# Key stages with both halves of the input side by side, and the bank's halves added on VectorE

## The chip, the cores and the metric

The kernel runs on one core of a Trainium2 chip. The metric is the device time of one execution in microseconds (us), as the median of several runs. A tile is 128 partitions high throughout; 512 f32 columns of the accumulation memory are one bank.

## The reference

Two transformer-like blocks are applied one after the other to 256 tokens of width 1024, in f32. The change is in the PEER layers of the first block, of which there are two (layer 0 and layer 1):

```python
def peer(h, w_q, sub_keys, u_emb, v_emb):
    # per block of 128 tokens x_t
    q = einsum('td,dhk->thk', x_t, w_q).reshape(T, 8, 2, 128)
    s = einsum('thpk,hpnk->thpn', q, sub_keys)
    sv, si = top_k(s, 16)                       # 16 best of 128 keys, for both halves
    cand = sv[:, :, 0, :, None] + sv[:, :, 1, None, :]
    fv, fpos = top_k(cand, 16)                  # 16 best of 256 sums
    gate = softmax(fv)
    act = gelu(einsum('thkd,td->thk', u_emb[eidx], x_t), approximate=False)
    return einsum('thk,thkd->td', gate * act, v_emb[eidx])
```

There are 16384 experts of width 1024 in each layer. The kernel does not gather the chosen rows: it computes the activation of every expert for every token, multiplies by a table of gates that is zero for experts not chosen, and multiplies the result with the whole of `v_emb`.

## The kernel before

f32 products are made of reduced-precision parts. A 128 x 1024 weight tile that arrives in `weight_raw` is rounded by ScalarE into `weight_high` (`make_high`, L272), and VectorE writes raw minus high over the raw tile as `weight_low` (`make_low`, L278). The input `h` is kept as `h_high` and `h_low` in the same way. A product (`product`, L382) is three matmuls: high weight with high input, high weight with low input, low weight with high input. There are four weight slots and four banks in use (`RING` = 4). SyncE loads tile n as soon as TensorE has finished tile n - 4 (`tiles_used`).

The stage that is changed is `peer_scores` (called the key stage here). It runs once in each layer, over 128 tiles of 128 experts. For every tile TensorE makes 8 blocks of three matmuls of 256 columns into one half of a bank, waiting for the weight's low part and for the bank (`bank_free`). What the others do in one step of the order written out by hand:

- ScalarE, step n: wait until tile n is multiplied (`tiles_used`); Gelu of bank n into `acts` (L1227), which also frees the bank; `make_high` of tile n + 3. After nine of the steps in a layer the Exp of a head's gates follows (L1236). In layer 0, after every fourth step from 15 on, it issues the DMA of a modulation block of 512 KB (`load_later_modulation`, L683), i.e. the one that VectorE uses in the next step of its own that has one. The first two blocks are loaded by SyncE at the start.
- VectorE, step n (from 3 on): `make_low` of tile n, which waits for `make_high` of tile n. In layer 0, where n >= 10 and n % 4 == 2, then one block of modulation work (L654, 128 x 1024), which waits for that block's DMA; 28 of them in the stage. In nine steps the sum, reciprocal and product for a head's gates (L1261 to L1263). Then as many of the 256 picking steps (`pick_experts`: 16 steps for each of 8 heads and two token groups) as are due: `done * PICKED_BY < n * 256`.
- GpSimd scatters the gates of seven heads to the table in HBM, one indirect DMA for each of 16 picks and head.

Each of these queues is executed strictly in this order. Behind the key stage lies `peer_weigh`, which builds what multiplies the second token group's activations, and `peer_output`, which multiplies with `v_emb` by matmuls of 512 columns (L1442).

The lines used below: L272 high part, L278 low part, L382 the matmuls of `product`, L592 `add_to_x` (VectorE adds a bank to an SBUF tile), L321 Square of such a tile on ScalarE, L654 and L683 modulation work and its DMA, L1087 to L1145 the picking, L1227 Gelu, L1236 Exp, L1442 the 512-column matmuls of the output stage.

Of the kernel before, what the change touches and what calls it, by code (L numbers as in the profile page):

```python
# [8 lines left out]
F32R = mybir.dt.float32r  # L9
I32 = mybir.dt.int32  # L10
U32 = mybir.dt.uint32
ALU = mybir.AluOpType
# [3 lines left out]
P = 128  # L16
D = 1024
KB = D // P
T = 256
# [142 lines left out]
class Core:  # L162


    def __init__(self, nc, dram):
        self.nc, self.dram = nc, dram
        sb = lambda name, shape, dt=F32: nc.alloc_sbuf_tensor(name, shape, dt)
        aligned = lambda: (nc.sbuf_base + 31) // 32 * 32

        def over(name, shape, dt, start):  # L170

            return nc.alloc_sbuf_tensor_at(name, shape, dt, offset=start)

        arena_at = aligned()
        self.arena = sb("arena", [P, P * T])
        self.x = sb("x_T", [P, KB, T])


        h_at = aligned()
        self.h_high = sb("h_high", [P, KB, T], F32R)  # L180
        self.h_low = sb("h_low", [P, KB, T], F32R)

        self.scratch = over("scratch", [P, 2 * KB * T], F32, h_at)
        self.act_high = over("act_high", [P, RING, T], F32R, h_at)
        self.act_low = over("act_low", [P, RING, T], F32R, h_at + RING * T * 4)

        self.mem_high = over("mem_high", [P, KB, T], F32R, arena_at + 4 * MEM_AT)
        self.mem_low = over("mem_low", [P, KB, T], F32R, arena_at + 4 * (MEM_AT + KB * T))

        self.hidden_high = over("hidden_high", [P, 32, T], F32R, arena_at + 4 * 10240)  # L190
        self.hidden_low = over("hidden_low", [P, 32, T], F32R, arena_at + 4 * 18432)

        raw_at = aligned()
        self.raw = sb("weight_raw", [P, RING, KB * P])
        self.low = over("weight_low", [P, RING, KB * P], F32R, raw_at)
        high_at = aligned()
        self.high = sb("weight_high", [P, RING, KB * P], F32R)

        self.spare = over("spare", [P, RING, KB * P], F32, high_at)
        self.work = sb("work", [P, 512])  # L200
        self.squares = sb("squares", [P, 2, T])
        self.kept = sb("kept", [P, 16 * T])
        self.kv = view(self.kept, 0, 16, T)
        self.later = view(self.kept, 0, 2, D)
        self.mem = view(self.kept, 0, KB, T)
        self.silu = self.kept[:, 2 * D:3 * D]
        self.gates = view(self.kept, 3 * D, RING, P)
        self.table = [nc.dram_tensor(f"gate_table{layer}", (P * P * P, 1), F32, kind="Internal").ap() for layer in range(2)]
        self.const = sb("const", [P, dram["resident"].shape[1]])
        self.cols = sb("cols", [P, dram["cols"].shape[1]])  # L210
        self.mod = sb("mod", [P, 2, 48])
        self.gain = sb("gain", [P, 4, KB])
        self.trig = sb("trig", [P, 4, T])
        self.pick = Picks(sb, self.kept[:, 3 * D + RING * P:4 * D].rearrange("p (t a b) -> p t a b", t=TT, a=TOPK))
        self.banks = nc.alloc_psum_tensor("bank", [P, 8 * BANK], F32)
        self.bank = [self.banks[:, i * BANK:(i + 1) * BANK] for i in range(8)]
        self.flags = {}
        self.segments = []
        self.next_segment = 0

    def sig(self, name):
        if name not in self.flags:
            self.flags[name] = Signal(self.nc, name)
        return self.flags[name]
# [151 lines left out]
    def product(self, out, slot, rhs, k, start, stop):  # L376
# [5 lines left out]
            mm = self.nc.tensor.matmul(out, w, x, start=(start and i == 0), stop=(stop and i == 2), skip_group_check=skip)  # L382
        return mm


    def linear(self, engine, take, groups=1, rhs=None, loads=(), aside=None, per_tile=1, norm=None, squares=None, root=None, aside_act=None, halves=None, first=None):

# [675 lines left out]


PICK_STEPS = 16
PICKED_BY = 104
GATED_BY = 112


def picked_at(h):  # L1070
# [112 lines left out]
def peer_scores(core, layer):  # L1183
# [2 lines left out]

    nc, sig = core.nc, core.sig
    used, free, step, picked = sig("tiles_used"), sig("bank_free"), sig("dve_step"), sig("experts_picked")
    exped, gated, turned, cleared = sig("gates_exped"), sig("gates_ready"), sig("turned"), sig("table_cleared")
    seg, k = core.take_segment()  # L1190
    following = core.segments[k + 1]
# [6 lines left out]
    with nc.Block() as block:  # L1198
        @block.sync
        def _(sp):  # L1200
            if layer == 0:
                sp.wait_ge(cleared.sem, 16 * CLEARINGS)
                for n in range(EARLY_MODS, EARLY_MODS + 2):
                    load_later_modulation(core, sp, n)
            core.stream(sp, seg, k)

        @block.tensor
        def _(pe):
            with pe.Fori(0, P // RING) as turn:
                for slot in range(RING):  # L1210

                    pe.wait_ge(free.sem, turn * RING + free.at(slot + 1 - RING))
                    core.wait_turn(pe, seg, turn, slot)
                    for c in range(KB):
                        mm = core.product(core.bank[slot][:, 0:T], slot, (core.h_high[:, c, :], core.h_low[:, c, :]), c,
                                          c == 0, c == KB - 1)
                    mm.then_inc(used.sem, 1)

            pe.wait_ge(gated.sem, gated.at(HEADS + 1))
            transposes(core, pe, [b.chosen[:, 1, 1, :]], [core.bank[4]], turned)  # L1220
            transposes(core, pe, [b.expo[:, 1].rearrange("p h k -> p (h k)")], [core.bank[5]], turned)

        @block.scalar
        def _(act):
            for n in range(P):
                act.wait_ge(used.sem, seg.first + RING + n + 1)
                nc.scalar.activation(acts[:, n, :], core.bank[n % RING][:, 0:T], ACT.Gelu).then_inc(free.sem, 1)  # L1227
                ahead = n + RING - 1
                if ahead < P:
                    core.make_high(act, seg, ahead - ahead % RING, ahead % RING)  # L1230
                else:
                    core.make_high(act, following, 0, ahead - P)
                if ahead in exp_at:
                    h = exp_at[ahead]
                    act.wait_ge(picked.sem, picked.at(h + 1))
                    nc.scalar.activation(gates(h), gates(h), ACT.Exp).then_inc(exped.sem, 1)  # L1236
                if layer == 0 and n % RING == RING - 1 and 3 <= n // RING < LATER // 2 + 3:
                    load_later_modulation(core, act, EARLY_MODS + n // RING - 1)

        @block.gpsimd  # L1240
        def _(pool):
            pool.wait_ge(cleared.sem, 16 * CLEARINGS * (layer + 1))
            scatter_gates(core, pool, layer, range(SCATTERED_EARLY))

        @block.vector
        def _(dve):

            link = Chain(step, dve)
            picking = (i for t in range(TT) for h in range(HEADS) for i in pick_experts(core, link, scores, t, h))
            steps = modulations(core, dve, range(EARLY_MODS, EARLY_MODS + LATER // 2))  # L1250
            done, all_steps = 0, TT * HEADS * PICK_STEPS
            for n in range(RING - 1, P):
                core.make_low(dve, seg, n - n % RING, n % RING)
                if layer == 0 and n >= 10 and n % RING == 2:
                    next(steps, None)
                if n in gate_at:
                    h = gate_at[n]
                    total = b.total[:, 0:1] if h < HEADS else b.total[:, HEADS:2 * HEADS]
                    of = gates(h)
                    dve.wait_ge(exped.sem, exped.at(h + 1))  # L1260
                    link(nc.vector.tensor_reduce(total, of, AX_X, ALU.add))  # L1261
                    link(nc.vector.reciprocal(total, total))
                    nc.vector.tensor_tensor(of, of, total.unsqueeze(2).to_broadcast(list(of.shape)), ALU.mult) \  # L1263
                        .then_inc(gated.sem, 1)
                while done < all_steps and done * PICKED_BY < n * all_steps:
                    next(picking)
                    done += 1
            step.used = link.n
            for n in range(RING - 1):
                core.make_low(dve, following, 0, n)  # L1270
            for n in range(2):
                dve.wait_ge(turned.sem, turned.at(n + 1))
                nc.vector.tensor_copy(b.by_pick[:, n, :], core.bank[4 + n][:, 0:P])
# [2 lines left out]
    picked.close(HEADS + 1)  # L1276
    exped.close(HEADS + 1)
    free.close(P)


WEIGHED_EARLY = 2
# [1426 lines left out]
```

## Time and profile before

| | value |
|---|---|
| median of 3 runs | 2740.25 us (2738.56 to 2741.69) |
| the profiled execution | 2738.82 us, of which the traced span is 2736.7 us |
| key stage of layer 0, from the low part of tile 3 to the last low part | 380.4 us |
| key stage of layer 1, the same | 366.1 us |
| mean granted TensorE clock | 0.965 of 2.4 GHz |

Of the page, part 1 is the busy time of each engine, part 2 the same in 40 slices of 68.4 us, and part 5 the groups of instructions. The two key stages lie in slices 4 to 9 and 19 to 24 (counted from 1): there TensorE (PE) is the busiest and VectorE (DVE) second. The busy time of PE counts overlapping matmuls once.

### The profile page before, as it was taken

The page shows a single profiled execution, that of the slowest core. Times are in us where ns is not written, and L with a number is a line of the kernel's source. Part 1 is how long each engine was busy: PE and PEld are TensorE (multiplying, and loading weights), DVE is VectorE, ACT ScalarE, POOL GpSimd, SP SyncE. Part 2 cuts the span into 40 slices and gives each one's busy share as a digit, 9 for nine tenths or more (in the row PEclk, how much of TensorE's full clock was granted, in tenths as well). Part 3 has the DMA queues.
Part 4 walks back from the last instruction along what each step waited for, and adds up shares of the span by engine and source line. Part 5 has one row for each costly group of instructions (what it writes and reads, how often), then busy time and mean ns, then how long its engine had stood idle before and what let it go on. Part 6 is the DMA issues. An engine that isn't in the chain of part 4 may idle for free. (4 is left out here: it accounts for less than half of the span.)

```text
span 2736.7 us, 45422 instructions
## 1 busy us (share of the span) xinstructions
PE 2511.7 (92%) x17052; PEld 2287.0 (84%) x17052; DVE 1858.1 (68%) x3789; ACT 1308.0 (48%) x1979; POOL 508.6 (19%) x320
## 2 busy tenths in 40 slices
PE   5698999999999999778999998999999988888998
PEld 4588999997888889468999997788888867777998
DVE  5676998858777774654888848666665566554754
ACT  3345554556444454344665456455545441044443
POOL 0001666623000000100576743000000010000000
PEclk8899999999999999789999999999999989999999
DMA  8755777762787765334777762677774530033554
GB/s 347 266 174 153 220 210 220 218 215 39 255 265 268 262 215 166 147 97 135 184 182 180 184 184 43 209 217 217 218 216 132 161 109 24 1 118 95 163 163 154
DMA packets 200510, 480.75 MB, mean 176 GB/s; under 512 B 54448, under 2 KB 87728, under 8 KB 199760
## 3 DMA queue, kind: packets, MB, share of 16 engines
q1 hardware_dynamic: 150960, 432.01, 49.9%
q10 hardware_dynamic: 12576, 47.29, 4.4%
q0 software_dynamic: 36864, 0.15, 3.4%
q8 instruction: 48, 0.79, 0.1%
q14 instruction: 62, 0.51, 0.1%
HBM read 461.41 MB, written 17.96 MB: 175 GB/s over the span
## 5 line engine op out<-in xcount | busy, mean ns | idle before, releaser
L278 DVE TENSOR_TENSOR weight_low<-weight_raw,weight_high 128x1024 fp32r<-128x1024 f32 x732 | 892.3, 1221 | 405.2 <-ACT weight_high L272 397.1
L272 ACT ACTIVATE weight_high<-weight_raw 128x1024 fp32r<-128x1024 f32 x732 | 773.9, 1059 | 663.8 <-DMA weight_raw<-peer_v_dram 336.8
L382 PE MATMUL bank<-h_high,weight_high 128*128 128x256 f32 x3424 | 984.0, 287 | 81.1 <-DVE weight_low L278 24.2
L382 PE MATMUL bank<-h_low,weight_high 128*128 128x256 f32 x3424 | 979.3, 286 | 0.0
L382 PE MATMUL bank<-h_high,weight_low 128*128 128x256 f32 x3424 | 978.9, 286 | 0.0
L382 PEld LDWEIGHTS bank<-h_high,weight_high 128*128 128x128 f32 x3424 | 668.3, 195 | 95.1 <-issue 80.8
L382 PEld LDWEIGHTS bank<-h_low,weight_high 128*128 128x128 f32 x3424 | 668.2, 195 | 0.0
L382 PEld LDWEIGHTS bank<-h_high,weight_low 128*128 128x128 f32 x3424 | 667.9, 195 | 0.0
L1161 POOL DMA_INDIRECT gate_table<-pick_expo,pick_spot x256 | 468.6, 1831 | 752.1 <-DVE pick_expo L1263 461.1
L1442 PE MATMUL bank<-weight_high,act_high 128*128 128x512 f32 x1024 | 316.6, 390 | 6.1 <-DVE act_low L1509 6.1
L1442 PE MATMUL bank<-weight_low,act_high 128*128 128x512 f32 x1024 | 316.8, 391 | 0.0
L1442 PE MATMUL bank<-weight_high,act_low 128*128 128x512 f32 x1024 | 316.2, 390 | 0.0
L1509 DVE TENSOR_TENSOR act_low<-arena,act_high 128x256 fp32r<-128x256 f32 x256 | 108.7, 424 | 213.5 <-ACT act_high L1476 212.8
L1442 PEld LDWEIGHTS bank<-weight_high,act_high 128*128 128x128 f32 x1024 | 192.6, 188 | 46.4 <-issue 6.4
L1442 PEld LDWEIGHTS bank<-weight_high,act_low 128*128 128x128 f32 x1024 | 193.1, 189 | 40.3
L1442 PEld LDWEIGHTS bank<-weight_low,act_high 128*128 128x128 f32 x1024 | 193.1, 189 | 40.1
L1227 ACT ACTIVATE arena<-bank 128x256 f32<-128x256 f32 x256 | 97.9, 383 | 224.0 <-PE bank L382 222.2
L1598 POOL TENSOR_TENSOR arena<-arena,trig 128x512 f32<-128x512 f32 x12 | 17.9, 1524 | 487.8 <-POOLq L398 487.8
L1476 ACT ACTIVATE act_high<-arena 128x256 fp32r<-128x256 f32 x256 | 102.3, 400 | 12.3 <-PEq L1301 11.6
L585 ACT ACTIVATE arena<-bank 128x256 f32<-128x256 f32 x108 | 41.2, 381 | 130.9 <-PE bank L382 130.9
L654 DVE SCALAR_TENSOR_TENSOR kept<-kept 128x1024 f32<-128x1024 f32 x56 | 68.4, 1221 | 25.0 <-DMA kept<-ada_later_dram 24.9
L1596 POOL MEMSET kept<- 128x1024 f32 x1 | 1.0, 951 | 454.1 <-SPq L1565 454.1
(342 smaller groups left out, 2691.8 us busy)
## 6 DMA issues: line engine op xcount, KB each, us to landing
weight_raw<-peer_u_dram SPq DMA_DIRECT2D x256, 512.0 KB
weight_raw<-peer_v_dram SPq DMA_DIRECT2D x256, 512.0 KB
kept<-ada_later_dram ACTq DMA_DIRECT2D x54, 512.0 KB
gate_table<-kept ACTq DMA_DIRECT2D x8, 2048.0 KB, 16.7
weight_raw<-peer_w_q_dram SPq DMA_DIRECT2D x32, 512.0 KB
kept<-gate_table SPq DMA_DIRECT2D x256, 64.0 KB, 3.4
weight_raw<-w_in_dram SPq DMA_DIRECT2D x32, 512.0 KB
weight_raw<-mlp_w_up_dram SPq DMA_DIRECT2D x32, 512.0 KB
```

Source lines behind the costliest of these rows:

```text
L272: self.nc.scalar.activation(self.high[:, slot, :], self.raw[:, slot, :], ACT.Identity) \
L278: eng.tensor_tensor(self.low[:, slot, :], self.raw[:, slot, :], self.high[:, slot, :].bitcast(F32), ALU.subtract) \
L382: mm = self.nc.tensor.matmul(out, w, x, start=(start and i == 0), stop=(stop and i == 2), skip_group_check=skip)
L585: return lambda n, bank: self.nc.scalar.activation(dst[:, n + offset, :], bank, func)
L654: i = nc.vector.scalar_tensor_tensor(out=block, in0=block, scalar=1.0, in1=core.silu[:], op0=ALU.mult, op1=ALU.mult, accum_out=mod[:, n:n ...
L1161: pool.indirect_dma_start(core.table[layer], bass.IndirectOffsetOnAxis(ap=b.spot[:, h, i:i + 1], axis=0), b.expo[:, 0, h, i:i + 1], None, ...
L1227: nc.scalar.activation(acts[:, n, :], core.bank[n % RING][:, 0:T], ACT.Gelu).then_inc(free.sem, 1)
L1442: mm = nc.tensor.matmul(out[2 * t + h][:], x[:, slot, of], w[:, slot, halves[h]], start=(first and n == 0), stop=(last and n == 2), skip_g ...
L1476: nc.scalar.activation(core.act_high[:, n % RING, :], acts[:, n, :], ACT.Identity).then_inc(rounded.sem, 1)
L1509: nc.vector.tensor_tensor(core.act_low[:, slot, :], acts[:, n, :], core.act_high[:, slot, :].bitcast(F32), ALU.subtract).then_inc(split.se ...
L1596: nc.gpsimd.memset(core.later[:, 0, :], 0.0).then_inc(sig("zeros_made").sem, 1)
L1598: nc.gpsimd.tensor_tensor(dst[:, 2 * n:2 * n + 2, :], src[:, 2 * n:2 * n + 2, :], cosb, ALU.mult) \
```

## The change

`h_high` and `h_low` become two views of one tile `h_parts`, in which the high and the low half of each of the 8 blocks of the input lie side by side: 512 columns. In the key stages the two matmuls with the high weight become one of 512 columns over the whole bank; the matmul with the low weight has 256 columns and adds to the bank's first half. In the last block of a tile the narrow one comes first. The two halves of a bank then have to be added: ScalarE copies the second half to `acts` (a new semaphore `halves_copied`), VectorE adds the first half to it, which frees the bank, and ScalarE's Gelu now works on `acts` in SBUF, one step later. `PICKED_BY` goes from 104 to 116 and `GATED_BY` from 112 to 122.

```diff
-        self.h_high = sb("h_high", [P, KB, T], F32R)
-        self.h_low = sb("h_low", [P, KB, T], F32R)
+        self.h_parts = sb("h_parts", [P, KB, 2, T], F32R)
+        self.h_high, self.h_low = self.h_parts[:, :, 0, :], self.h_parts[:, :, 1, :]
...
+    def side_by_side(self, bank, slot, k):
+
+        high, low = self.high[:, slot, k * P:(k + 1) * P], self.low[:, slot, k * P:(k + 1) * P]
+        parts, last = self.h_parts[:, k], k == KB - 1
+        wide = lambda: self.nc.tensor.matmul(bank[:], high, parts.rearrange("p s t -> p (s t)"), start=(k == 0), stop=last,
+                                             skip_group_check=True)
+        narrow = lambda: self.nc.tensor.matmul(bank[:, 0:T], low, parts[:, 0, :], start=False, stop=False, skip_group_check=True)
+        if last:
+            narrow()
+            return wide()
+        wide()
+        return narrow()
...
-PICKED_BY = 104
-GATED_BY = 112
+PICKED_BY = 116
+GATED_BY = 122
...
                     for c in range(KB):
-                        mm = core.product(core.bank[slot][:, 0:T], slot, (core.h_high[:, c, :], core.h_low[:, c, :]), c,
-                                          c == 0, c == KB - 1)
+                        mm = core.side_by_side(core.bank[slot], slot, c)
...
         @block.scalar
         def _(act):
+            def activate(n):
+                act.wait_ge(free.sem, free.at(n + 1))
+                nc.scalar.activation(acts[:, n, :], acts[:, n, :], ACT.Gelu)
+
             for n in range(P):
                 act.wait_ge(used.sem, seg.first + RING + n + 1)
-                nc.scalar.activation(acts[:, n, :], core.bank[n % RING][:, 0:T], ACT.Gelu).then_inc(free.sem, 1)
+                nc.scalar.activation(acts[:, n, :], core.bank[n % RING][:, T:2 * T], ACT.Identity).then_inc(copied.sem, 1)
+                if n:
+                    activate(n - 1)
                 ahead = n + RING - 1
                 if ahead < P:
                     core.make_high(act, seg, ahead - ahead % RING, ahead % RING)
...
+            activate(P - 1)
...
+            def add(n):
+                dve.wait_ge(copied.sem, copied.at(n + 1))
+                nc.vector.tensor_tensor(acts[:, n, :], core.bank[n % RING][:, 0:T], acts[:, n, :], ALU.add).then_inc(free.sem, 1)
+
             for n in range(RING - 1, P):
                 core.make_low(dve, seg, n - n % RING, n % RING)
+                add(n - RING + 1)
...
             for n in range(RING - 1):
                 core.make_low(dve, following, 0, n)
+                add(P - RING + 1 + n)
```

## Rows read from the trace of the kernel before

**Rows 1.** Windows: both key stages, then 100 us of layer 1's key and output stages.

```profile
core 0: us, PE busy (x) PEld busy (x) DVE busy (x) ACT busy (x) POOL busy (x), PEclk, DMA share, GB/s
230.88:611.32 380.44, 369.40 (x3039) 365.44 (x3037) 319.66 (x828) 205.46 (x281) 209.41 (x112) 1.00 0.75 214
1288.58:1654.68 366.10, 364.59 (x3039) 364.35 (x3037) 286.72 (x772) 206.26 (x281) 209.41 (x112) 1.00 0.72 182
...
1400.00:1500.00 100.00, 100.00 (x835) 100.00 (x835) 85.60 (x249) 56.71 (x78) 68.06 (x37) 1.00 0.74 181
...
1800.00:1900.00 100.00, 100.00 (x443) 82.81 (x442) 65.44 (x114) 51.76 (x78) 0.00 (x0) 1.00 0.71 217
```

**Rows 2.** Waits in layer 0's key stage: who waited for whom, total us, times, longest.

```profile
DVE kept L654 <- DMA kept<-ada_later_dram: 24.9, 23, 2.2
```

**Rows 3.** Timeline of both engines in a later stage that adds banks to SBUF.

```profile
2438.84 1.06 ACT L272 ACTIVATE weight_high<-weight_raw 128x1024 fp32r<-128x1024 f32 x1 [1.23 <-DMA weight_raw<-xattn_w_q_dram]
...
2439.93 1.22 DVE L278 TENSOR_TENSOR weight_low<-weight_raw,weight_high 128x1024 fp32r<-128x1024 f32 x1 [0.70 <-ACT weight_high L272]
2441.08 0.41 DVE L330 TENSOR_TENSOR work<-work,squares 128x256 f32<-128x256 f32 x1
2441.41 0.42 DVE L592 TENSOR_TENSOR x_T<-bank,x_T 128x256 f32<-128x256 f32 x1
...
2441.86 0.42 ACT L321 ACTIVATE squares<-x_T 128x256 f32<-128x256 f32 x1 [1.65 <-DVE x_T L592]
```

**Rows 4.** Instructions by line: duration min/median/max in ns, of Square from SBUF.

```profile
L321 ACT ACTIVATE squares<-x_T x40: 397/401/418, 133.3 to 2728.4; 128x256 f32<-128x256 f32 x40
```

**Rows 5.** Timeline of VectorE in layer 1's key stage (start, duration, line, form).

```profile
1289.72 0.48 DVE L1087 MAX8 pick_top<-arena 128x8 f32<-128x128 f32 x2
...
1293.87 1.21 DVE L278 TENSOR_TENSOR weight_low<-weight_raw,weight_high 128x1024 fp32r<-128x1024 f32 x1
```

**Rows 6.** Timeline around an Exp, layer 1's key stage: ScalarE, and VectorE behind it.

```profile
1345.07 0.21 ACT L1236 ACTIVATE pick_expo<-pick_expo 128x16 f32<-128x16 f32 x1
1345.30 1.28 ACT L1227 ACT_TABLE_LOAD   x1
1346.59 0.38 ACT L1227 ACTIVATE arena<-bank 128x256 f32<-128x256 f32 x1
1346.87 1.05 ACT L272 ACTIVATE weight_high<-weight_raw 128x1024 fp32r<-128x1024 f32 x1
...
1348.03 1.23 DVE L278 TENSOR_TENSOR weight_low<-weight_raw,weight_high 128x1024 fp32r<-128x1024 f32 x1 [1.54 <-ACT weight_high L272]
```

**Rows 7.** Timeline, layer 0: three modulation blocks, the DMA's issue and VectorE's use.

```profile
419.74 0.34 ACTq L683 DMA_DIRECT2D kept<-ada_later_dram  x1
...
425.17 1.23 DVE L654 SCALAR_TENSOR_TENSOR kept<-kept 128x1024 f32<-128x1024 f32 x1 [1.92 <-DMA kept<-ada_later_dram]
...
493.18 0.33 ACTq L683 DMA_DIRECT2D kept<-ada_later_dram  x1
...
497.01 1.23 DVE L654 SCALAR_TENSOR_TENSOR kept<-kept 128x1024 f32<-128x1024 f32 x1 [0.51 <-DMA kept<-ada_later_dram]
...
575.84 1.06 ACT L272 ACTIVATE weight_high<-weight_raw 128x1024 fp32r<-128x1024 f32 x1 [0.34 <-DMA weight_raw<-peer_u_dram]
575.85 0.33 ACTq L683 DMA_DIRECT2D kept<-ada_later_dram  x1
...
580.13 1.22 DVE L654 SCALAR_TENSOR_TENSOR kept<-kept 128x1024 f32<-128x1024 f32 x1 [1.98 <-DMA kept<-ada_later_dram]
```

**Rows 8.** Windows with TensorE partly idle, and the clock granted in them.

```profile
2328.00:2340.00 12.00, 9.04 (x115) 8.58 (x112) 7.01 (x13) 0.00 (x0) 3.83 (x16) 1.00 0.01 2
...
609.00:621.00 12.00, 8.08 (x45) 6.95 (x44) 7.85 (x22) 7.95 (x15) 6.18 (x4) 0.86 0.28 64
```

**Rows 9.** Timeline of TensorE: the idle stretch behind layer 0's key stage.

```profile
613.79 0.48 PE L1322 MATMUL bank<-spread_by,pick_firsts 128*128 128x512 f32 x1 [3.92 <-ACT spread_by L1345]
```

More of the change, by code:

```diff
@@ L1188, in peer_scores @@
     used, free, step, picked = sig("tiles_used"), sig("bank_free"), sig("dve_step"), sig("experts_picked")
+    copied = sig("halves_copied")
     exped, gated, turned, cleared = sig("gates_exped"), sig("gates_ready"), sig("turned"), sig("table_cleared")
@@ L1278, in peer_scores @@
     free.close(P)
+    copied.close(P)
 WEIGHED_EARLY = 2
```

## The prediction

> **What bounds the kernel now.** I read the page's slices first: both key stages show TensorE full and VectorE at 60 to 90%. Then the windows [rows 1]. In layer 1's key stage TensorE is busy 364.6 of 366.1 us at the full clock of 2.4 GHz: it is the bound. 835 matmuls of 256 columns in 100 us are 119.8 ns each, so a tile of 24 takes 2.874 us, and 127 tiles 365 us. In layer 0 the stage is 380.4 us long with the same matmuls; VectorE is busy 319.7 us there, against 286.7, because of 28 modulation blocks, and it also waits 23 times, 24.9 us in all, for their DMA [rows 2]. VectorE is near its limit there, and the stage is bound by TensorE in some tiles and by VectorE in others. The GpSimd scatter is busy 209 us of either and ends before it.
>
> What matters most is not in any busy share: how the queues hang together. Before, ScalarE's step n needs only TensorE's tile n and a loaded weight; VectorE's step needs ScalarE's high part. Nothing on ScalarE waits for VectorE, but for an Exp that follows its picks by two tiles. So an engine that falls behind in one tile can catch up in the next.
>
> **TensorE's part of the change.** A matmul of 512 columns costs 100 us / 443 = 225.7 ns [rows 1] (in the output stage, same reduced-precision type, full clock). A block is then 225.7 + 119.8 = 345.5 ns instead of 359.3, a tile 2.764 us instead of 2.874: 0.110 us less, 14 us in each layer, if TensorE remained the bound. The Trainium skill ("TensorE: Matmul & The Clock Gate", section "Wait — 56ns, not 53.3ns?") gives a fixed cost of about 2.5 ns for each matmul at the full clock, by which the saving would be 2.5 ns x 8 x 128 x 2 = 5 us in all. The rows say otherwise: two narrow ones minus one wide are 13.9 ns, and I go by them.
>
> **The new loop.** ScalarE's step m is now: copy of bank m, Gelu of m - 1, high part of m + 3. That Gelu waits for VectorE's addition m - 1, which stands in VectorE's queue behind the low part of m + 2, which waits for the high part of m + 2, which stands behind ScalarE's Gelu of m - 2. So one turn of a ring through both engines is needed for each tile, and no buffer loosens it. Its terms, from a stage where the same forms follow each other [rows 3]: low part to the start of the next on VectorE 1.15 us (2439.93 to 2441.08, I take 1.14); addition from a bank 0.42; end of it to the start on ScalarE 0.03 to 0.05 (2441.83 to 2441.86); Gelu from SBUF as Square from SBUF, 0.40 [rows 4], of which 0.10 overlaps the next instruction: 0.30 (Gelu from a bank shows 0.28 to the next high part [rows 6]); high part 1.06; to VectorE 0.03 (2439.90 to 2439.93). I take 0.04 and 0.06 for the two crossings, as one in the key stage is 0.11 (1347.92 to 1348.03) [rows 6]. Sum 1.14 + 0.42 + 0.04 + 0.30 + 1.06 + 0.06 = **3.02 us**, over TensorE's 2.76. The loop takes the bound: 127 turns are 383.5 us. TensorE isn't in it: tile m is multiplied some 4.1 us after the start of its low part, and the copy of it has until 5.9 us (two turns less 0.1). The copy itself (0.28 to the next instruction) lies in ScalarE's gap of 1.66 us while VectorE makes low part and addition, and costs nothing; with that gap gone it would cost 0.28.
>
> **What hangs on VectorE.** After the addition has started, VectorE has 3.02 - 1.14 - 0.34 = 1.54 us for the rest before the next high part is there. Picking: the first 8 steps take 1289.72 to 1293.87 = 4.15 us [rows 5]. In all of layer 1's stage VectorE is busy 286.7 us [rows 1], 156 of it with 128 low parts of 1.22; with the 0.04 us that a step waits for its forerunner, some 250 times, the 256 steps are 141 us. The rule gives 7 steps in the first tile (3.7 us of work, +2.2 us over a turn), then two or three a tile, 1.21 us on average. They fit but where three long ones meet: +3.2 us by going through the schedule. PICKED_BY at 116 costs nothing by itself, as the gates for the last transposes are due at 122 of 128.
>
> **Exp.** Nine times in a layer ScalarE puts a table load of 1.28, the Exp of 0.21 and another table load of 1.28 into its queue (the Exp and the load behind it stand in [rows 6]). Before, that was covered by ScalarE's idle time. Now 1.28 + 0.24 + copy 0.28 + 1.28 = 3.08 must fit in the gap of 1.66: 1.42 over, x 9 = +12.8 us. The bounds are 0 (the loads elsewhere) and that.
>
> Layer 1: 383.5 + 2.2 + 3.2 + 12.8 = **401.7** against 366.1, +35.6 us.
>
> **Modulation blocks in layer 0.** Block i is asked for in ScalarE's step 4i + 7, behind the high part of tile 4i + 10, and used in VectorE's step 4i + 10. The last one: issue 575.85, use 580.13, 4.28 us later; two earlier ones, with the scatter beside them, took 5.43 (419.74 to 425.17) and 3.83 us (493.18 to 497.01), the longest and the shortest of the 23 that were waited for [rows 7]. VectorE waited 1.1 us on average before, since it was otherwise behind ScalarE and the block had had time. In the loop it is never behind: the issue comes with the Gelu's start, 1.40 us before the low part starts, and VectorE is ready for the block 1.48 after. With 4.5 us for the DMA it waits until 3.10, 1.62 us each. A tile with a block takes 3.10 + 1.15 + 1.21 = 5.46 instead of 3.02: +2.44, x 26 = 63.4 us; the two blocks loaded at the start cost 0.8 each, 1.6. Less what coincides (three of the Exp excesses 4.3, picks that are already counted 0.7, the last block without picks 1.3): 58.7. Layer 0: 401.7 + 58.7 = **460.4** against 380.4, +80.0 us.
>
> **Ends.** The next stage starts 0.3 us later than before in relation to the last low part (one addition), the first tile is 0.1 us shorter, in both layers: +0.4. The strided `h_high` and `h_low` elsewhere are rows of 256 as before: 0. Sum: 80.0 + 35.6 + 0.4 = **+116 us**, from the profiled 2738.8 to 2854.8; that execution lies 1.4 us under the median. I predict 2855.
>
> **Bounds.** Crossings at 0.03 both: -6 us, at 0.11 both: +20. DMA at 3.8: -18, at 5.4: +23. Exp hidden: -20. The forecast's own range is 2830 to 2890.
>
> **Rivals.**
> 1. The loop holds but the modulation DMA is hidden (it lands within 2.9 us, because less is moved in a us): tile with a block 1.48 + 1.15 + 1.21 = 3.84, layer 0 about 421, time 2738.8 + 40 + 36 = 2815 to 2818. Against it: no block of the trace was used under 3.8 us after its issue where VectorE waited. Chance 0.12.
> 2. Faster: TensorE stays the bound. It decides when a turn of the loop is under 2.76 us, that is if 0.26 us of its terms overlapped across engines; then 14 us go in each layer, 2711. For it speaks only that TensorE is the bound now and has less to do; against it, every term is a row, and semaphores put them in sequence. Also here lies the case that it is near zero because the loop costs what the matmuls save. Chance 0.04 faster, 0.02 even. In layer 0 the modulation would undo it in part.
> 3. The clock. TensorE would be busy 2.76 of 3.0 to 5.5 us, idle up to 2.7 at a time. The rows have 75% busy at full clock, and a fall after an idle stretch of 3.92 us [rows 8, 9]. If it fell in a third of layer 0's tiles, a tile there takes 8 x (225.7 + 119.8) x 2 = 5.5 us, about 1.9 over the mean 3.6: +80 us, 2935. The Trainium skill (the same page, "A second HAM failure mode: psum-queue depth-cycling") describes a clock that oscillates where TensorE idles briefly between groups; the rows here don't bear that out for gaps under 3 us. Chance 0.09.
> 4. The wide matmul isn't cheaper than two narrow ones: TensorE's tile stays 2.87, still under 3.02, and nothing changes in the time. It is inside the forecast.
>
> **Chances.** Forecast 0.70 (2830 to 2890), hidden DMA 0.12, clock 0.09, faster 0.04, even 0.02, slower otherwise 0.03. The range for 8 in 10 takes in the first two: 2812 to 2890. A difference under 0.2% (5.5 us) can't be told from none: faster 0.04, same 0.02, slower 0.94.
>
> **What would show it.** In the profile after: 512-column matmuls at 226 ns apart, gaps of TensorE before each tile that end with the low part; the low parts 3.0 us apart in layer 1 with VectorE waiting for the high part and ScalarE's Gelu waiting for the addition (about 1.2 us each time); 4.4 us where an Exp lies; in layer 0 every fourth interval over 5 us, with VectorE waiting about 40 us in all for `kept<-ada_later_dram`; stages of about 460 and 402 us. Wrong if the low parts follow each other by less than 2.9 us, if the modulation wait doesn't grow, or if the granted clock in the stages is under 1.00.

## The result and the profile after

The changed kernel takes 2863.48 us (median of 4, 2858.77 to 2864.55) against 2740.92; the ratio is 1.0445, 95% interval 1.0427 to 1.0463. The profiled execution took 2864.51 us, with a span of 2862.7 us, 126.0 more than before.

The first view is the windows of both key stages, from the low part of tile 3 to the last one, and of 100 us inside layer 1's, as in [rows 1]. Columns: us, then busy time (and instructions) of PE, PEld, DVE, ACT and POOL, the granted clock, DMA share and GB/s.

```profile
231.26:693.87 462.61, 391.67 (x2026) 321.09 (x2025) 363.46 (x954) 234.97 (x409) 198.49 (x112) 0.96 0.63 177
1376.85:1779.29 402.44, 382.13 (x2028) 308.40 (x2026) 329.24 (x898) 234.39 (x409) 195.68 (x112) 1.00 0.65 167
1450.00:1550.00 100.00, 92.39 (x489) 74.09 (x488) 84.67 (x244) 61.63 (x106) 68.36 (x41) 1.00 0.67 160
```

Layer 0's stage grew from 380.4 to 462.6 us (+82.2), layer 1's from 366.1 to 402.4 (+36.3). That is 118.5 of the 126.0. TensorE has gaps now, VectorE has more work but isn't full (329 of 402 us), and ScalarE is busy 58% of the time in layer 1. TensorE is still shown as busy 95% of layer 1's stage, but that alone doesn't make it the bound: e5 below lengthens its work on a tile, and the stage stays as it is. What binds, only the waits show. These are the largest of layer 1's stage between the engines of the chain, and then the ones of layer 0's; GpSimd's waits and those of the weight loads are left out (us in total, times, longest):

```profile
ACT arena L1240 <- DVE arena L1274: 164.4, 116, 1.9
DVE weight_low L278 <- ACT weight_high L272: 71.2, 81, 7.5
```

```profile
ACT arena L1240 <- DVE arena L1274: 227.2, 119, 4.5
PE bank L390 <- DVE weight_low L278: 65.4, 38, 3.1
DVE weight_low L278 <- ACT weight_high L272: 56.4, 66, 7.4
DVE kept L667 <- DMA kept<-ada_later_dram: 40.9, 26, 2.1
```

ScalarE's Gelu (now L1240) waits for VectorE's addition (L1274), and VectorE's low part for ScalarE's high part: two engines that wait for each other in turn. Before, the Gelu waited for TensorE (222.2 us in both layers). The wait for the modulation DMA grew from 24.9 us [rows 2] to 40.9. Some turns of the ring in layer 1, first VectorE's lines, then ScalarE's:

```profile
1502.21 1.23 DVE L278 TENSOR_TENSOR weight_low<-weight_raw,weight_high 128x1024 fp32r<-128x1024 f32 x1 [0.23 <-ACT weight_high L272]
1503.35 0.42 DVE L1274 TENSOR_TENSOR arena<-bank,arena 128x256 f32<-128x256 f32 x1
...
1505.28 1.23 DVE L278 TENSOR_TENSOR weight_low<-weight_raw,weight_high 128x1024 fp32r<-128x1024 f32 x1 [0.56 <-issue]
```

```profile
1503.81 0.42 ACT L1240 ACTIVATE arena<-arena 128x256 f32<-128x256 f32 x1 [1.43 <-DVE arena L1274]
1504.13 1.04 ACT L272 ACTIVATE weight_high<-weight_raw 128x1024 fp32r<-128x1024 f32 x1
1505.08 0.36 ACT L1244 ACTIVATE arena<-bank 128x256 f32<-128x256 f32 x1
1506.87 0.42 ACT L1240 ACTIVATE arena<-arena 128x256 f32<-128x256 f32 x1 [1.43 <-DVE arena L1274]
```

Low part 1502.21, addition 1503.35 to 1503.77, Gelu 1503.81, high part 1504.13 to 1505.17, next low part 1505.28: 3.07 us. The profile names no releaser for the wait before that last one (`issue`), but the high part had ended 0.11 us before it. These are the same terms as were taken from [rows 3], in a stage where they formed no ring.

### The profile page after: what moved, and what is told of

It is laid out like the page before. It is cut to its first block and busy times, and to the rows that moved or that the text cites. A ratio compares the mean times of both kernels' runs of the same rounds, so it can differ in the third digit from the quotient of the medians.

```text
span 2862.7 us, 41854 instructions
## 1 busy us (share of the span) xinstructions
PE 2556.2 (89%) x15004; PEld 2186.5 (76%) x15004; DVE 1945.4 (68%) x4045; ACT 1363.5 (48%) x2235; POOL 484.6 (17%) x320
## 5 line engine op out<-in xcount | busy, mean ns | idle before, releaser
L390 PE MATMUL bank<-h_parts,weight_high 128*128 128x512 f32 x2048 | 766.4, 412 | 94.8 <-DVE weight_low L278 79.1
L1174 POOL DMA_INDIRECT gate_table<-pick_expo,pick_spot x256 | 444.1, 1735 | 898.4 <-DVE pick_expo L1288 467.9
L382 PE MATMUL bank<-h_parts,weight_high 128*128 128x256 f32 x2752 | 516.6, 290 | 58.0 <-DVE h_parts L548 20.8
L390 PEld LDWEIGHTS bank<-h_parts,weight_high 128*128 128x128 f32 x2048 | 391.0, 192 | 226.9 <-issue 140.6
L392 PE MATMUL bank<-h_parts,weight_low 128*128 128x256 f32 x2048 | 540.6, 284 | 0.0
L382 PEld LDWEIGHTS bank<-h_parts,weight_high 128*128 128x128 f32 x2752 | 444.7, 199 | 68.7 <-issue 61.3
L392 PEld LDWEIGHTS bank<-h_parts,weight_low 128*128 128x128 f32 x2048 | 395.9, 193 | 13.7
L382 PE MATMUL bank<-h_parts,weight_low 128*128 128x256 f32 x1376 | 397.7, 289 | 0.0
L1240 ACT ACTIVATE arena<-arena 128x256 f32<-128x256 f32 x256 | 107.1, 418 | 394.9 <-DVE arena L1274 391.6
L382 PEld LDWEIGHTS bank<-h_parts,weight_low 128*128 128x128 f32 x1376 | 272.9, 198 | 0.0
L1469 PEld LDWEIGHTS bank<-weight_high,act_low 128*128 128x128 f32 x1024 | 193.4, 189 | 40.3
L1503 ACT ACTIVATE act_high<-arena 128x256 fp32r<-128x256 f32 x256 | 102.3, 400 | 12.3 <-PEq L1328 11.6
L1274 DVE TENSOR_TENSOR arena<-bank,arena 128x256 f32<-128x256 f32 x256 | 107.0, 418 | 0.0
L598 ACT ACTIVATE arena<-bank 128x256 f32<-128x256 f32 x108 | 41.3, 382 | 132.1 <-PE bank L382 132.1
```

Of the source, the lines that this page charges most:

```text
L390: wide = lambda: self.nc.tensor.matmul(bank[:], high, parts.rearrange("p s t -> p (s t)"), start=(k == 0), stop=last, skip_group_check=True)
L392: narrow = lambda: self.nc.tensor.matmul(bank[:, 0:T], low, parts[:, 0, :], start=False, stop=False, skip_group_check=True)
L598: return lambda n, bank: self.nc.scalar.activation(dst[:, n + offset, :], bank, func)
L1174: pool.indirect_dma_start(core.table[layer], bass.IndirectOffsetOnAxis(ap=b.spot[:, h, i:i + 1], axis=0), b.expo[:, 0, h, i:i + 1], None, ...
L1240: nc.scalar.activation(acts[:, n, :], acts[:, n, :], ACT.Gelu)
L1274: nc.vector.tensor_tensor(acts[:, n, :], core.bank[n % RING][:, 0:T], acts[:, n, :], ALU.add).then_inc(free.sem, 1)
```

## The experiments

Stage lengths are read as above in each kernel's own trace, from the low part of tile 3 to the last low part. All are variants of the changed kernel, but e6, which is one of the kernel before. Stages are of one profiled execution each.

| kernel | layer 0's stage | layer 1's stage | median us |
|---|---|---|---|
| before | 380.4 | 366.1 | 2740.9 |
| changed | 462.6 | 402.4 | 2863.5 |
| e1_high_first | 420.7 | 358.5 | 2774.4 |
| e2_mod_early | 422.3 | 402.4 | 2820.9 |
| e3_no_tables | 456.8 | 390.8 | 2845.0 |
| e5_narrow_halves | 464.9 | 402.4 | 2864.1 |
| e8_short_gelu | 458.9 | 391.8 | 2844.7 |
| e7_both | 379.5 | 358.6 | 2732.3 |
| e4_wide_alone | 372.7 | 358.5 | 2725.5 |
| e6_before_mod_early | 367.5 | 366.1 | 2727.9 |
| e9_layer1_only | 365.9 | 358.3 | 2718.8 |
| e10_wide_early | 360.2 | 358.4 | 2712.4 |

**Breaking the ring (e1_high_first).** Two instructions change places in ScalarE's order:

```diff
                 nc.scalar.activation(acts[:, n, :], core.bank[n % RING][:, T:2 * T], ACT.Identity).then_inc(copied.sem, 1)
-                if n:
-                    activate(n - 1)
                 ahead = n + RING - 1
                 if ahead < P:
                     core.make_high(act, seg, ahead - ahead % RING, ahead % RING)
                 else:
                     core.make_high(act, following, 0, ahead - P)
+                if n:
+                    activate(n - 1)
```

> The changed kernel, but in ScalarE's step n the high part of tile n + 3 is issued ahead of the Gelu of tile n - 1. Theory (a ring of Gelu, high part, low part, addition, one turn of 3.02 us for each tile): the ring then spans two tiles, some 1.6 us each, and no longer binds. TensorE's 2.76 us and VectorE's 2.69 us of own work do: layer 1's stage about 355 us instead of 402.4, layer 0's about 390 instead of 462.6 (modulation DMA still partly waited for), the whole about 2745 us. Rival (VectorE is simply full with the additions, or the wide matmuls are slow): the order on ScalarE changes little, over 2830 us.

2774.4 us, ratio to the kernel before 1.0116 (1.0087 to 1.0145). In layer 1 the stage falls from 402.4 to 358.5 us with exactly the same instructions. A window and the two waits of its stage show what binds now:

```profile
1400.00:1500.00 100.00, 100.00 (x569) 86.93 (x568) 96.83 (x281) 74.76 (x122) 68.05 (x36) 1.00 0.75 185
```

```profile
ACT arena L1244 <- PE bank L390: 48.8, 96, 1.5
...
ACT arena L1240 <- DVE arena L1274: 5.0, 12, 0.7
```

TensorE is busy throughout, the copy waits for TensorE, and the Gelu's wait for the addition has gone from 164.4 to 5.0 us. ScalarE also waits 55.1 us there for the weight tiles, whose slots TensorE frees. The ring is shown to be the cause in layer 1: with it broken, the stage takes the same 358.5 us as without additions and copies (e4 below), so these cost nothing there. In layer 0, 420.7 us were measured where about 390 were expected. Its waits name the rest:

```profile
DVE kept L667 <- DMA kept<-ada_later_dram: 41.2, 26, 2.7
```

**Earlier modulation DMA (e2_mod_early).**

```diff
-                if layer == 0 and n % RING == RING - 1 and 3 <= n // RING < LATER // 2 + 3:
-                    load_later_modulation(core, act, EARLY_MODS + n // RING - 1)
+                if layer == 0 and n % RING == RING - 1 and 2 <= n // RING < LATER // 2 + 2:
+                    load_later_modulation(core, act, EARLY_MODS + n // RING)
```

> The changed kernel, with each modulation block's DMA in the key stage issued four tiles earlier. Theory: the 26 waits of VectorE for it, 40.9 us, go: layer 0's stage about 424 us instead of 462.6, layer 1's stays at 402.4, the whole about 2825. Rival (the DMA lands late because the queues are full, however early it is issued, or the wait covers something else that then comes to light): under 10 us gained.

2820.9 us. Layer 0's stage is 40.3 us shorter, for a wait of 40.9 that is gone from the waits; layer 1's is the same to 0.1 us. So nothing covers that wait. How it came about, in the changed kernel (ScalarE's issue, VectorE's wait):

```profile
401.64 0.42 ACT L1240 ACTIVATE arena<-arena 128x256 f32<-128x256 f32 x1 [1.43 <-DVE arena L1274]
401.65 0.34 ACTq L696 DMA_DIRECT2D kept<-ada_later_dram  x1
```

```profile
403.36 1.22 DVE L278 TENSOR_TENSOR weight_low<-weight_raw,weight_high 128x1024 fp32r<-128x1024 f32 x1
404.50 0.42 DVE L1274 TENSOR_TENSOR arena<-bank,arena 128x256 f32<-128x256 f32 x1
406.46 1.23 DVE L667 SCALAR_TENSOR_TENSOR kept<-kept 128x1024 f32<-128x1024 f32 x1 [1.54 <-DMA kept<-ada_later_dram]
```

The issue goes out with the Gelu, the block is used 4.81 us later, and VectorE stands for 1.54 us of it. Behind it stand the tile's picking steps and the next low part.

**No table loads (e3_no_tables).**

```diff
-                    nc.scalar.activation(gates(h), gates(h), ACT.Exp).then_inc(exped.sem, 1)
+                    nc.scalar.activation(gates(h), gates(h), ACT.Gelu).then_inc(exped.sem, 1)
```

> The changed kernel with the Exp of the gates replaced by a Gelu, so that ScalarE loads no other table in the key stages (the gates' values are left out by that, all waits stay). Theory (1.42 us of each Exp step sticks out of ScalarE's gap of 1.66 us): layer 1's stage 12 us shorter, 390; layer 0's 8 us shorter, since three of nine fall beside a modulation wait; the whole about 2843. Rival (the loads are covered by the gap): no change, 2863.

2845.0 us; layer 1's stage 11.6 us shorter, layer 0's 5.8, where 12 and 8 were expected. Nine Exp steps cost 1.3 us each in layer 1; before the change TensorE was busy 364.6 of 366.1 us there, so they can hardly have cost anything. In the changed kernel one of them looks like this:

```profile
1397.25 1.28 ACT L1255 ACT_TABLE_LOAD   x1
1398.54 0.21 ACT L1255 ACTIVATE pick_expo<-pick_expo 128x16 f32<-128x16 f32 x1
1398.66 0.37 ACT L1244 ACTIVATE arena<-bank 128x256 f32<-128x256 f32 x1
1399.05 1.28 ACT L1240 ACT_TABLE_LOAD   x1
1400.34 0.42 ACT L1240 ACTIVATE arena<-arena 128x256 f32<-128x256 f32 x1
```

The addition was done at 1398.82; the Gelu starts 1.52 us later, when the queue in front of it is done.

**One term of the ring (e8_short_gelu).**

```diff
-                nc.scalar.activation(acts[:, n, :], acts[:, n, :], ACT.Gelu)
+                nc.scalar.activation(acts[:, n, 0:P], acts[:, n, 0:P], ACT.Gelu)
```

> The changed kernel with the Gelu of the key stages made on 128 of its 256 columns (the second token group's activations keep their value before the Gelu; that part is left out). One term of the ring becomes shorter, from 0.42 to about 0.30 us. Theory (each term of the ring counts one for one in each tile): layer 1's stage 0.12 x 127 = 15 us shorter, 387; layer 0's about 12 shorter, 451; the whole about 2836. Rival (VectorE or TensorE binds, ScalarE is idle half the time and its work is covered): no change, 2863.

The Gelu of 128 columns takes 0.311 us instead of 0.418, and layer 1's stage is 10.6 us shorter, 0.083 a tile for a term that shrank by 0.107. So the term counts, though not fully one for one: ScalarE is idle 1.4 us before each of these Gelus, and its work sets the time all the same. Turn by turn, 92 of the 127 became shorter by about the whole term (0.09 us or more) and 26 hardly at all (under 0.05). The latter fit tiles in which VectorE's picking takes longer than the rest of the ring, as between 1500.55 and 1502.11 of this run, where the next low part followed the picking without a wait. In layer 0 only 3.7 of the expected 12 us came. The 25 turns there that take over 4.6 us because of a modulation block became 4.7 us longer together, the others 8.5 us shorter. The wait for the block's DMA grew from 40.9 to

```profile
DVE kept L667 <- DMA kept<-ada_later_dram: 45.7, 26, 2.5
```

Part of that growth is expected, as VectorE comes to the block earlier after the issue while the DMA takes as long; part is what this wait differs by between kernels with the same Gelu (43.7 us in the next one).

**TensorE's rate (e5_narrow_halves, e4_wide_alone).** The first makes the wide matmul of two narrow ones:

```diff
-        wide = lambda: self.nc.tensor.matmul(bank[:], high, parts.rearrange("p s t -> p (s t)"), start=(k == 0), stop=last,
-                                             skip_group_check=True)
+        def wide():
+            self.nc.tensor.matmul(bank[:, 0:T], high, parts[:, 0, :], start=(k == 0), stop=last, skip_group_check=True)
+            return self.nc.tensor.matmul(bank[:, T:2 * T], high, parts[:, 1, :], start=False, stop=last, skip_group_check=True)
```

> The changed kernel with its wide matmul made as two of 256 columns into the two halves of the bank, all else as changed. TensorE then needs 2.88 us for a tile instead of 2.82, still under the ring's 3.02 to 3.06. Theory (the ring binds, TensorE's rate doesn't matter): stages of 402 and 463 us, the whole 2863, within 3. Rival (TensorE is still the bound, with stalls of its own in the wide matmuls): 8 us slower in each layer or, if the wide ones stall, faster.

2864.1 us, layer 1's stage 402.35 against 402.44: with or without the wide matmul the changed kernel takes the same time. (Layer 0's stage is 2.3 us longer, with 2.8 us more of waiting for the modulation DMA.) The second takes the price away and leaves the matmuls:

```diff
-                nc.scalar.activation(acts[:, n, :], core.bank[n % RING][:, T:2 * T], ACT.Identity).then_inc(copied.sem, 1)
-                if n:
-                    activate(n - 1)
+                nc.scalar.activation(acts[:, n, :], core.bank[n % RING][:, 0:T], ACT.Gelu).then_inc(free.sem, 1)
...
-                add(n - RING + 1)
...
-                add(P - RING + 1 + n)
```

> The matmuls of the changed kernel alone, with the order of the kernel before: Gelu reads the first half of the bank and frees it; the copy, the addition and with them the product of the high weight and the low input are left out. It measures what the wide matmuls save where nothing is paid for them. By the matmul rows (345.5 ns for a block instead of 359.3) layer 1's stage is 127 x 2.764 = 351 us instead of 366.1, layer 0's about 370, the whole about 2715. By a rule of 2.5 ns for each matmul saved it would be 363 in layer 1 and the whole about 2735.

2725.5 us, ratio 0.9939 (0.9917 to 0.9962). Layer 1's stage is 358.5 us, 7.6 less than before, where 15 were expected. In layer 1's window, 569 matmuls in 100 us are 16 in 2.812 us, so a block takes 351.5 ns, neither the 345.5 of the rows nor what two narrow ones take (359.3). In the timeline of this kernel a wide one is followed after 0.23 to 0.24 us, a narrow one after 0.12:

```profile
1501.36 0.40 PE L390 MATMUL bank<-h_parts,weight_high 128*128 128x512 f32 x1
1501.59 0.28 PE L392 MATMUL bank<-h_parts,weight_low 128*128 128x256 f32 x1
1501.71 0.40 PE L390 MATMUL bank<-h_parts,weight_high 128*128 128x512 f32 x1
1501.95 0.28 PE L392 MATMUL bank<-h_parts,weight_low 128*128 128x256 f32 x1
```

So even free of charge, the wide matmuls are worth 15 us in the two layers together, 0.6%.

**Both edits (e7_both), and the control (e6_before_mod_early).** The first is e1 and e2 together, the second is e2's edit in the kernel before.

> The changed kernel with both edits: ScalarE's high part ahead of the Gelu, and the modulation DMA four tiles earlier. Theory (ring and DMA wait are all that makes the change slower): layer 1's stage 358.5 as with the first edit alone, layer 0's bound by VectorE's own work, some 3.0 us a tile, about 385; the whole about 2735 to 2738, level with the kernel before and some us over that kernel with the early DMA. Rival (something else in layer 0 is slower, as its 421 us with the first edit alone could mean): layer 0's stage stays over 400, the whole over 2750.

> The kernel before, with each modulation block's DMA in the key stage issued four tiles earlier, as in the changed kernel's variant with the same edit. Theory: the 24.9 us that VectorE waited for it go, but two thirds of them lay in tiles where TensorE was the bound: layer 0's stage 380.4 becomes about 373, layer 1's stays 366, the whole 2733. Rival (those waits were all covered): no change, 2740.

e7_both: 2732.3 us, ratio 0.9969 (0.9959 to 0.9979). Its stages are 379.5 and 358.6 us. So without the ring and the DMA wait the changed kernel is no slower than the one before: 83.1 + 43.8 us have gone from the two stages by reordering alone. Layer 0 needed both: either edit by itself left about 421. e6: 2727.9 us, ratio 0.9952 (0.9932 to 0.9972), layer 0's stage 12.9 us shorter where 7 were expected. The kernel before already paid for that late DMA, and against e6, the fair comparison, e7 is still 12 us behind in layer 0's stage and 4 us in the whole.

**What holds layer 0 then (e10_wide_early), and the best of both (e9_layer1_only).** e10 is e4 with the early DMA. e9 is e7 with, in layer 0, the three narrow matmuls and the Gelu from the bank:

```diff
-                        mm = core.side_by_side(core.bank[slot], slot, c)
+                        if layer == 0:
+                            mm = core.product(core.bank[slot][:, 0:T], slot, (core.h_high[:, c, :], core.h_low[:, c, :]), c,
+                                              c == 0, c == KB - 1)
+                        else:
+                            mm = core.side_by_side(core.bank[slot], slot, c)
...
+                if layer == 0:
+                    nc.scalar.activation(acts[:, n, :], core.bank[n % RING][:, 0:T], ACT.Gelu).then_inc(free.sem, 1)
```

> The wide matmuls in the order of the kernel before (copy, addition and with them the product of the high weight and the low input left out), with the modulation DMA four tiles earlier. It tells what holds layer 0's stage at 379.5 us where both edits are made. Theory (the additions fill VectorE there): without them TensorE is the bound and the stage takes 358 to 361 us, layer 1's 358.5; the whole 2714. Rival (the DMA or GpSimd's scatter holds it): 370 or more.

> Both edits (high part ahead of the Gelu, modulation DMA four tiles earlier), and the wide matmuls with their copy and addition in layer 1 alone; layer 0 is multiplied and put out as before. Theory: layer 1's stage 358.6 us as with both edits, layer 0's 367 as in the kernel before with the early DMA; the whole 2720, that is 0.7% under the kernel before and 8 us under the kernel before with the early DMA. Rival (the layers influence each other, or the gain of the wide matmuls in layer 1 is given back behind the stage): 2727 or more.

e10: layer 0's stage 360.2 us. With the additions and copies (e7) it is 379.5, so the two together cost 19.3 us there; neither the DMA nor GpSimd's scatter, which are in both, holds it over 360. The windows of layer 0 in e7, and of e9's two stages:

```profile
300.00:500.00 200.00, 191.41 (x1057) 161.30 (x1056) 194.14 (x533) 127.07 (x214) 131.40 (x70) 1.00 0.79 218
```

```profile
231.05:596.94 365.89, 364.59 (x3039) 364.35 (x3037) 318.12 (x827) 206.17 (x281) 207.51 (x112) 1.00 0.78 223
1275.15:1633.49 358.34, 356.87 (x2027) 310.08 (x2025) 327.42 (x899) 246.68 (x409) 207.59 (x112) 1.00 0.73 186
```

In e7 VectorE is busy 97% of those 200 us: in layer 0 it is nearly full, and there the additions are real work in the path. In layer 1 it has more room (busy 327.4 of 358.3 us in e9), and they are free. e9 uses that: 2718.8 us, ratio 0.9917 (0.9904 to 0.9931), faster than both kernels and 9 us faster than e6. The two were measured at different times; the kernel before took 2742.3 us beside e9 and 2742.6 beside e6.

## Why the prediction was right

Foretold were 2855 us, between 2830 and 2890; measured were 2863.5.

- **The new loop.** Foretold 3.02 us a turn and 401.7 us for layer 1's stage; measured 2.99 to 3.07 in 109 of 127 turns, 3.04 on the mean, and 402.4. e1 shows the cause, e5 that TensorE's rate has no part in it, e8 that ScalarE's term has. That the sum comes so close is in part luck: the turns brought 2.3 us more than foretold and the long picking steps 1.6 less.
- **Exp.** Foretold +12.8 us in layer 1; e3 gives 11.6.
- **Modulation.** Foretold 1.62 us of waiting for each of 26 blocks, 42.1 in all; measured 40.9, and e2 got 40.3 back. A turn with one of them: foretold 5.46, 5.47 on the mean. Here two terms were off and cancelled: from issue to use it is 4.7 us instead of 4.5, and VectorE comes to the block 3.1 us after the issue instead of 2.9. Layer 0's stage: foretold 460.4, measured 462.6. Rival 1 (DMA hidden) fell: it would have been e2's 422 us.
- **Picking.** The first turn of 5.21 us was foretold at 3.02 + 2.2. That PICKED_BY costs nothing was not tested by itself; e9's layer 0, with 116, takes 365.9 us and e6's, with 104, 367.5.
- **TensorE's part.** This term was mis-sized: 0.110 us a tile foretold, 0.06 measured (e4). Two rows of unlike stages were put together, and a wide matmul beside a narrow one isn't one among wide ones. It did no harm, as TensorE wasn't the bound. The 2.5 ns a matmul of the Trainium skill ("TensorE: Matmul & The Clock Gate", section "Wait — 56ns, not 53.3ns?") would have given 0.02 us a tile, as an estimate. The 7.8 ns that a block saves here (e4) lies between that and the 13.9 ns of the rows.
- **Rival 2 (faster).** Its mechanism, TensorE as the bound, is what e1 made of layer 1. It only needed the ring broken, and its prize was half of what had been put down.
- **Rival 3 (clock).** The prediction named a granted clock under 1.00 in the stages as a sign of being wrong, and in layer 0 that sign came: 0.96 on the mean, where it was 1.00. On this point the forecast was wrong, though it hardly shows in the time. The lowest window of 20 us, and TensorE's two long waits in it:

```profile
440.00:460.00 20.00, 16.26 (x74) 13.48 (x75) 15.62 (x47) 10.96 (x18) 13.46 (x8) 0.85 0.57 147
```

```profile
440.75 0.77 PE L390 MATMUL bank<-h_parts,weight_high 128*128 128x512 f32 x1 [2.67 <-DVE weight_low L278]
457.02 0.47 PE L390 MATMUL bank<-h_parts,weight_high 128*128 128x512 f32 x1 [2.71 <-DVE weight_low L278]
```

  In the whole stage TensorE stood 15 times for 2.2 to 3.1 us, and the clock fell to half around the end of ten of these waits. By its rows the prediction had not expected a fall for gaps under 3 us; most of these are shorter. With the DMA waits gone (e2) the longest of TensorE's waits inside the stage was 1.5 us and the clock at 1.00 again. What the falls cost was not measured apart, but it is little: the stage came out only 2.2 us over the sum, and e2, without them, is shorter by no more than the DMA wait.
- **Ends.** Here the sum was short. 126.0 us were measured, 116 foretold; the stages make 2.9 of the difference. Some 7 us lie behind them. A part is named: behind layer 0's key stage TensorE now stands 7.17 us instead of 3.92 [rows 9], and its matmuls run at half clock from the first on (0.42 to 0.43 us apart), where before the first three still ran faster,

```profile
693.50:703.50 10.00, 6.78 (x34) 5.71 (x34) 6.98 (x21) 6.53 (x14) 5.75 (x4) 0.69 0.12 0
```

  which by the eighth of them makes about 1 us. It is the same 7.17 us in e2, and 4.26 us in e1, so it seems to belong to the ring. Some 4 us come between layer 0's output stage and the end of the attention stage, whose code didn't change but for the place of `h_low`. That place is not the cause: the same stretch is 2.6 us longer in e6, which has the old place, and as before in e7, which has the new one. What makes it differ stays open.

## What to carry to other kernels

Before splitting a step over two in-order engines, follow the waits once round: if B's result feeds A and A's next instruction feeds B, the turn's length is a bound, whatever the busy shares say. Putting the instruction that others wait for ahead of the one that itself waits won back 44 us in layer 1's stage here. A DMA issued shortly before its use is covered only as far as the user is late; once the user keeps pace, it waits for the rest, here 1.6 of 4.7 us for each block. And such an edit has to be tried in the kernel before as well: e6 alone is faster than e7.

## What the runs showed of the hardware

- A 512-column matmul that alternates with a 256-column one takes about 0.235 us to the next start (e4), against 0.2257 among its own kind [rows 1]. Why was not tested.
- ScalarE's table load for the next function started as soon as the queue in front was done: at 1399.05 in the changed kernel it began 0.02 us behind the end of the copy, and the Gelu 0.01 us behind the end of the load.
- In the changed kernel the granted clock fell around the end of ten of TensorE's 15 waits of 2.2 to 3.1 us in layer 0's key stage (0.85 over the lowest 20 us). It stayed at 1.00 in layer 1's, where a turn leaves TensorE idle for some 0.2 us (3.04 less 2.81) and the longest wait was 1.5 us.
